# Delta-rule scan of a two-block network: where a unit's first VectorE operations stand, and when masks, end-decay products, transposes and the values' product are issued

## The reference

```python
def _rwkv7_scan(r, w, k, v, kk, a):
    def step(S, inp):
        r_t, w_t, k_t, v_t, kk_t, a_t = inp
        sa = -jnp.einsum('nhvk,nhk->nhv', S, kk_t)
        S = S * w_t[:, :, None, :] + sa[..., None] * (kk_t * a_t)[:, :, None, :] + v_t[..., None] * k_t[:, :, None, :]
        return S, jnp.einsum('nhvk,nhk->nhv', S, r_t)
```

## Time and profile before

| | us |
|---|---|
| median of 3 runs | 2951.4 |
| lowest, highest | 2947.35, 2955.93 |
| profiled execution, its time | 2956.71 |
| profiled execution, its span | 2954.9 |
| the scan of the delta rule, from about 455 to 700 of the span | 245 |

### The profile page before, as it was taken

The page is one execution under the profiler, slowest core; times in us unless marked ns, Lnnn a source line. Parts: engine busy times, 40 slices in busy tenths (PEclk is TensorE's granted clock), DMA queues, the critical chain, the costliest instruction groups (busy, mean ns, idle before and its releaser), DMA issues.

```text
span 2954.9 us, 41669 instructions
## 1 busy us (share of the span) xinstructions
PE 2779.1 (94%) x16834; PEld 2127.0 (72%) x16834; DVE 1735.8 (59%) x3143; ACT 1140.5 (39%) x2006; POOL 209.1 (7%) x212
## 2 busy tenths in 40 slices
PE   7999897789999999999988998999999998999998
PEld 4888766775666666666645776888888775788887
DVE  4256886565767777767647787433334687443333
ACT  3332244222256556555622327422223327432222
POOL 0000000000012222122200020000000030000000
PEclk9999897899999999999999999999999998999999
DMA  6210001434279889889976340323313240222412
GB/s 230 86 57 22 1 1 46 120 90 148 95 266 346 345 339 349 337 333 356 356 290 244 97 111 1 117 62 122 100 68 128 91 116 12 86 80 73 140 55 74
DMA packets 186541, 442.37 MB, mean 150 GB/s; under 512 B 21283, under 2 KB 110694, under 8 KB 167014
## 3 DMA queue, kind: packets, MB, share of 16 engines
q1 hardware_dynamic: 161862, 396.59, 37.3%
q0 software_dynamic: 24480, 43.04, 4.9%
HBM read 426.43 MB, written 38.29 MB: 157 GB/s over the span
## 4 chain that ended last, share of the span: by engine, by line
PE 78%; DVE 9%; DMA 7%; ACT 4%; issue 2%; POOL 0%; SPq 0%; POOLq 0%; DVEq 0%; ACTq 0%
PE ps L296 18%; PE ps L298 18%; PE ps L297 18%; PE ps L2502 6%; DMA hg<-h_rows,idx 3%; PE ps L2018 2%; DMA ring<-in_ew 2%; PE ps L1509 2%; PE ps L2528 2%; PE ps L2741 1%; DVE Pb L3488 1%; PE ps L2222 1%; PE ps L3393 1%; PE ps L586 1%; DMA yr<-y_rows 1%
## 5 line engine op out<-in xcount | busy, mean ns | idle before, releaser
L2953 DVE TENSOR_TENSOR wf<-ring,wf 128x1024 fp32r<-128x1024 f32 (+1 forms) x152 | 181.7, 1197 | 310.5 <-ACT wf L2949 310.1
L2949 ACT ACTIVATE wf<-ring 128x1024 fp32r<-128x1024 f32 (+1 forms) x152 | 156.8, 1033 | 343.3 <-PE ps L298 343.3
L296 PE MATMUL ps<-hxh,wf 128*128 128x512 f32 (+1 forms) x736 | 280.6, 381 | 2.3 <-DVE hxl L3116 2.3
L297 PE MATMUL ps<-hxl,wf 128*128 128x512 f32 (+1 forms) x736 | 280.3, 381 | 0.0
L298 PE MATMUL ps<-hxh,wf 128*128 128x512 f32 (+1 forms) x736 | 280.2, 381 | 0.0
L2440 DVE TENSOR_TENSOR spA<-ring,spA 128x1024 fp32r<-128x1024 f32 x156 | 184.7, 1221 | 105.5 <-ACT spA L2435 104.8
L2502 PE MATMUL ps<-ring,hdT 128*128 128x512 f32 x520 | 239.5, 604 | 0.8 <-issue 0.8
L2435 ACT ACTIVATE spA<-ring 128x1024 fp32r<-128x1024 f32 x156 | 158.3, 1055 | 53.0 <-DMA ring<-in_ew 42.5
L2502 PEld LDWEIGHTS ps<-ring,hdT 128*128 128x128 f32 x520 | 95.6, 194 | 97.2 <-issue 94.8
L2440 DVE TENSOR_TENSOR spB<-ring,spB 128x1024 fp32r<-128x1024 f32 x104 | 124.1, 1222 | 69.5 <-ACT spB L2435 69.5
L296 PEld LDWEIGHTS ps<-hxh,wf 128*128 128x128 f32 x736 | 139.1, 189 | 28.7 <-DVE hxl L3116 2.8
(11 more groups left out here) (621 smaller groups left out, 6181.7 us busy)
## 6 DMA issues: line engine op xcount, KB each, us to landing
ring<-in_ew SPq DMA_DIRECT2D x65, 2048.0 KB
ring<-in_ew SPq DMA_DIRECT2D x65, 1024.0 KB
ring<-in_w_in SPq DMA_DIRECT2D x17, 2048.0 KB, 8.9
ring<-in_w_gate SPq DMA_DIRECT2D x20, 1024.0 KB, 5.5
ring<-in_w_up SPq DMA_DIRECT2D x20, 1024.0 KB, 8.0
ring<-in_w_down SPq DMA_DIRECT2D x16, 1024.0 KB, 5.0
adaw<-in_ada_w SPq DMA_DIRECT2D x24, 512.0 KB, 6.2
ring<-in_w_out SPq DMA_DIRECT2D x6, 2048.0 KB, 8.1
```

Of the source, the lines that this page charges most:

```text
L296: pe.matmul(o, lhs[0], rhs[0], start=start, stop=False)
L297: pe.matmul(o, lhs[0], rhs[1], start=False, stop=False)
L2949: act.activation(item_part(n)[0], item_raw(n), ACT.Copy).then_inc(*w_hi.inc(n))
L2953: v.tensor_tensor(item_part(n)[1], item_raw(n), f(item_part(n)[0]), ALU.subtract).then_inc(*w_lo.inc(n))
```

## The change

Three edits, in DVE's, PE's and ACT's parts of the scan:

- `id` and `r0` of unit i+1 are issued on DVE at the end of unit i, in each direction's last step, right behind its `yo`. Before, each direction issued them at the head of unit i+1, ahead of its own `AT`. Unit 0's stand behind its `rows`.
- The masks `Bm`, `Ab`, `Ak` and the products `od2`, `od3` are issued on DVE behind level 1 instead of ahead of it.
- On PE the transposes `tr` follow U2 instead of U1, and `bv` follows U3 instead of U2; the copies on ACT move with them (`opE`, `opO` behind X2, `bv` behind X4).

```diff
-    q_pe = [Signal(sem(f"rw_mm{d}"), rw_keys(d, "c", "p2 p3 X1 U1 tr X2 U2 bv X3 U3" + " X4 U4" * d,
+    q_pe = [Signal(sem(f"rw_mm{d}"), rw_keys(d, "c", "p2 p3 X1 U1 X2 U2 tr X3 U3 bv" + " X4 U4" * d,
...
-    q_act = [Signal(sem(f"rw_scalar{d}"), rw_keys(d, "e ep dt", "X1 opE opO X2 X3 bv" + " X4" * d, "X4 " * (1 - d) + "X5 u0 TK")) for d in range(2)]
+    q_act = [Signal(sem(f"rw_scalar{d}"), rw_keys(d, "e ep dt", "X1 X2 opE opO X3" + " X4 bv" * d, "X4 bv " * (1 - d) + "X5 u0 TK")) for d in range(2)]
...
-                if k == 1:
+                if k == 2:
                     pe.wait_ge(*PV.val((u, "od3")))
...
-                if k == 2:
+                if k == 3:
                     pe.wait_ge(*PA.val((u, "opE")))
...
-                if k == 3:
+                if k == 4:
                     act.wait_ge(*P.val((u, "bv")))
...
-                if k == 1:
+                if k == 2:
                     act.wait_ge(*P.val((u, "tr")))
...
+        def start(i):
+            u, pu = (i, d), (i - 1, d)
+            if i:
+                v.wait_ge(*P.val((pu, "TK")))
+            v.tensor_copy(four(TT), bcm(C("cid"), 4)).then_inc(*PV.inc((u, "id")))
+            if i >= 2:
+                if i > 2:
+                    v.wait_ge(*P.val((pu, "y1")))
+                v.tensor_tensor(OPC[:, 0, :, :], rwm[:, 0:2, ORD[d][i] * 128:(ORD[d][i] + 1) * 128], E3[:, :, 0, :],
+                                ALU.mult).then_inc(*PV.inc((u, "r0")))
         v.wait_ge(*z_act.val("gsq"))
         rows(0)
+        start(0)
         yield
...
-            if i:
-                v.wait_ge(*P.val((pu, "TK")))
-            v.tensor_copy(four(TT), bcm(C("cid"), 4)).then_inc(*PV.inc((u, "id")))
-            if x:
-                if i > 2:
-                    v.wait_ge(*P.val((pu, "y1")))
-                v.tensor_tensor(OPC[:, 0, :, :], rwm[:, 0:2, tok], E3[:, :, 0, :], ALU.mult).then_inc(*PV.inc((u, "r0")))
...
             yield
-            mask(1, 1, f"ce_{d}", BTm, "Bm")
-            if x:
-                mask(0, 0, f"ci_{d}", Abt, "Ab")
-                mask(1, 0, f"ci_{d}", Akt, "Ak")
-            v.wait_ge(*PA.val((u, "dt")))
...
             yield
             for k in range(1, 6):
                 if k < 5:
                     aof(k + 1)
                 level(k)
                 yield
+                if k == 1:
+                    mask(1, 1, f"ce_{d}", BTm, "Bm")
+                    if x:
+                        mask(0, 0, f"ci_{d}", Abt, "Ab")
+                        mask(1, 0, f"ci_{d}", Akt, "Ak")
+                    v.wait_ge(*PA.val((u, "dt")))
...
                 if k < 5:
                     yield
...
+                if n and i < 5:
+                    start(i + 1)
                 yield
```

More of the change, by code:

```diff
@@ L1486, in rw_keys @@
         return out
-    q_pe = [Signal(sem(f"rw_mm{d}"), rw_keys(d, "c", "p2 p3 X1 U1 tr X2 U2 bv X3 U3" + " X4 U4" * d,
+    q_pe = [Signal(sem(f"rw_mm{d}"), rw_keys(d, "c", "p2 p3 X1 U1 X2 U2 tr X3 U3 bv" + " X4 U4" * d,
                                                 "X4 U4 " * (1 - d) + "X5 U5 u0 TK sa0 h0 ~y0 sa1 h1 ~y1"))
             for d in range(2)]
-    q_act = [Signal(sem(f"rw_scalar{d}"), rw_keys(d, "e ep dt", "X1 opE opO X2 X3 bv" + " X4" * d, "X4 " * (1 - d) + "X5 u0 TK")) for d in range(2)]
-    q_dve = [Signal(sem(f"rw_vector{d}"), rw_keys(d, "k1 k2 k3", "id ~r0 AT T0 TT0 Tm0 A1 Bm ~Ab ~Ak od2 od3 A2 TT1 Tm1 A3 TT2 Tm2 A4 TT3 Tm3 "
+    q_act = [Signal(sem(f"rw_scalar{d}"), rw_keys(d, "e ep dt", "X1 X2 opE opO X3" + " X4 bv" * d, "X4 bv " * (1 - d) + "X5 u0 TK")) for d in range(2)]
+    q_dve = [Signal(sem(f"rw_vector{d}"), rw_keys(d, "k1 k2 k3", "id ~r0 AT T0 TT0 Tm0 A1 A2 TT1 Tm1 Bm ~Ab ~Ak od2 od3 A3 TT2 Tm2 A4 TT3 Tm3 "
                                                   "A5 TT4 Tm4 TT5", "sa0 hq0 hd0 sa1 hq1 hd1 ~yo")) for d in range(2)]
@@ L1752, in rw_dve @@
                 yield
+                if k == 1:
[4 more added lines that the diff above has]
+                    v.wait_ge(*PA.val((u, "dt")))
+                    for a in range(2):
+                        v.tensor_tensor(OPD[:, a, :, :].rearrange("p q (c t) -> p (q c) t", c=2),
+                                        OPC[:, 2 + a, :, :].rearrange("p q (c t) -> p (q c) t", c=2), bc(Dt[:, i % 2, :], 64),
+                                        ALU.mult).then_inc(*PV.inc((u, f"od{2 + a}")))
                 if k < 5:
```

## The result

| | before | after |
|---|---|---|
| median, us | 2953.52 (6 runs, 2947.35 to 2958.59) | 2934.23 (6 runs, 2930.6 to 2936.48) |
| ratio to before, 95% interval | | 0.9942 [0.9927, 0.9956] |
| span of the profiled execution | 2954.9 | 2928.8 |
| the scan in that profile, `Tm0` of d = 1 in unit 0 to the last `yo` | 234.71 | 215.77 |

The changed kernel is faster: 17 us by the ratio, 13 to 22 by its interval (19 by the two medians). The forecast was 12.0 us and 2939.4, so the sign and the place were right and the gain was larger than forecast: it lies above the interval of 9 to 16 us that the prediction's main case gave. In the two profiles the scan alone is 18.9 us shorter.

A forecast was written before the change was run, and what follows sets the result against it. It took the hand-over between DVE and PE at the unit heads as the bound. Heads 15.2 us less 3.2 for levels 1 to 3 gave 12.0, from a median of 2951.4 to 2939.4 us; range 2932 to 2947.

The forecast's parts named there:

- the prediction's main case: Whole kernel: 12.0 us gained, 2939.4 us; interval 9 to 16 us, chance 0.61.
- What bounds the kernel: Unit heads: neither engine full; PE waits 16.1 us for r0 and 11.1 for A1, a hand-over between DVE and PE.
- the order is worth nothing: Rival: PE's work bounds the stretch, 198 of 245 us busy, so the time stays 2951; chance 0.06.
- The heads: Start of each unit: early id and r0 shorten the hand-over, 15.2 us gained over all units.
- Levels 1 and 2: Per unit, 9.83 us before: 9.0 at full clock, gain 0.8; 10.4 at half clock, loss 0.6.
- Level 3: Per unit: bv behind U3 delays d = 1 by 0.65 and exceeds TT3 and Tm3 by 0.26, loss 0.9 us.
- -3.2 us for levels 1 to 3 in units 2 to 5: Loss of 0.8 us in each of four units, with half of the units at the half clock.
- Units 0 and 1, taken at 0: Levels there: unit 1 +1.2 us at full clock or -1.5 at half, unit 0 1.5 either way; both counted as 0.
- The clock never falls: Rival: PE's clock stays full in the scan, 16.7 us gained, 2934.7 us; chance 0.08.
- Levels give more back: Rival: clock falls in every unit, levels cost 2.5 us a unit, 5 us gained, 2946 us; chance 0.20.
- The clock stays down to the unit's end: Rival: clock falls at the head and stays low, +12.8 us a unit, 2987 us; chance 0.05.
- What would show it: Trace after: r0 wait under 3 us, masks and bv on the chain, scan's end some 12 us earlier.

The follow-up runs named there:

- start_d0: The changed kernel with id and r0 of d = 1 put back at the unit's head; ratio to before 0.9979, scan 226.10 us.
- after_fill2: The changed kernel with unread products on PE in units 2 to 5, three and five; ratio to before 0.9931, scan 216.75 us.
- before_fill2: The kernel before with unread products, 9 and 5, behind PE's rows at heads of units 2 to 5; ratio 0.9987, scan 230.05 us.

## Why the prediction was right, and where it was off

**What bounds the kernel: right.** The hand-over between DVE and PE at the head, not either engine's load. The rival that said that the order is worth nothing, because PE bounds the stretch, fell: no product was taken away and the kernel gained 17 us. I had put it down to the Trainium skill's rule for the most occupied engine ("Perfetto Trace Analysis", "Identifying the Most-Contended Engine"), and that read too much into it. The section says which engine to work on first, and for TensorE it wants MFU and the share of the weight loads, not of the matmuls. By that share PE comes first here too, at 175 of 245 us against DVE's 155. It doesn't say that such an engine's waits for another are worth nothing, and the gain did come out of PE's waits: the 27 us for `r0` and `A1` are 13.6 after. DVE's instructions were only the means.

**The heads: right, and close unit by unit.** The gain in the table above stands in the row of the unit before.

| head of unit | 1 | 2 | 3 | 4 | 5 | sum |
|---|---|---|---|---|---|---|
| forecast, us | 0.2 | 3.2 | 3.8 | 3.3 | 4.5 (3.8) | 15.0 (of 15.2; unit 0's 0.2 lies ahead of the scan) |
| measured, us | 0.19 | 3.42 | 3.91 | 4.01 | 4.55 | 16.1; 15.9 with -0.14 in unit 5's own end |

Unit 3's stretch from the last y to X1 was forecast at 5.7 us and is 5.64. `start_d0` shows the reason given for it, that d = 1's rows hide behind `AT` to `A1` of d = 0: with only that half undone 10.3 us come back. Taken from the last y to X1 of d = 1 alone, unit 3 gained 3.9 and unit 4 3.5 (621.17 to 630.19 before, 609.38 to 614.87 after). Unit 2, from its state update to X1, took 6.58 us instead of 10.7, 4.2 gained: its rows ran at the full clock (1.14 us), for which the prediction had 3.9. That the table's 3.42 lies by the 3.2 of the half clock is luck; 0.7 were lost earlier in that step, 0.3 of them in a longer pause of PE (0.72 against 0.44).

**Levels 1 and 2: the sum was right, the weights were not.** At the full clock 9.0 was forecast, and unit 2 has 8.92 from X1 of d = 1 (540.16) to X3 (549.08). At the half clock 10.4 was forecast, and unit 3 has 9.73 (577.18 to 586.91), because the clock was back after 3 us, not after the whole two levels. The masks are on the chain and the transposes off it, as said. Three things were off. Where I took the clock to fall in half of the units, it fell in one of units 2 to 5 in the first profile (unit 3) and in units 3 and 5 in the second. Where it fell, the unit was still 0.1 shorter than before in levels 1 and 2, and not 0.6 longer. And I took unit 3, 9.83 us, for all units of before; by the transposes unit 3 has 10.09, and units 2 and 5 10.35 and 10.37, so they had more to gain (1.2 each).

**Level 3: the mechanism was right, the size twice too large.** 0.9 us a unit forecast, 0.47 measured in units 1 to 4 and none in unit 5; unit 0, taken at nothing, grew by 2.2. I had priced the eight products at a group of their own (0.65) on d = 0 plus 0.26 on d = 1. Back to back with U3 they cost 0.47, and d = 1's are hidden.

**The term of the sum that failed is -3.2 us for levels 1 to 3 in units 2 to 5.** Measured from the table: +0.70, -0.38, +0.27 and +1.19, together +1.8, which is 5.0 us better. Units 0 and 1, taken at 0, gave +0.4 and +0.8. With 0.7 more from the heads that is the 6.9 us between 12.0 forecast and 18.9 in the scan. The kernel's ratio puts the whole at 17 [13, 22], so the forecast lies 1 us below the interval. The measured median, 2934.23, lies in the range of 2932 to 2947 because its lower end was set for the rival in which the clock never falls, and what carried the time there was in part another thing, the levels' sign. That much was luck; the heads, 15.9 of the 18.9 us, for the most part were not.

**The rivals.** "The clock never falls", 16.7 us, is nearest in size, but not in its reason: `after_fill2` is that case, made true, and gained nothing over the change. With the clock full throughout, levels 1 to 3 of its units 2 to 5 are 2.6 us shorter than before, where the rival's sum had them 0.4 longer. What I had missed was more in the size of the levels than in the clock. "Levels give more back" is refuted: no unit of the kernel after has levels 1 and 2 longer than before, in either profile, and with level 3 the worst is unit 3 with 0.4 us lost, not 2.5. "The clock stays down to the unit's end" is refuted: the clock is 1.00 from 580 to the end of unit 3. What I held for certain and was wrong is that the half clock is dear in the old order; `before_fill2`, which kept it up most of the time, shows 4 us for the whole kernel.

**What would show it.** The wait for `r0` under 3 us: it is 0.7. `bv` on the chain in level 3: yes. All behind the scan shifted by the same: the load behind it moved from 699.69 to 678.49, 21.2 us, of which the scan explains 18.9 and the work ahead of it 2.3. `ada`'s loads were costed at nothing; its 64 products stand at the same step, and no wait for a load is among PE's largest waits.

## What to carry to other kernels

Where two engines hand work to each other and neither is full, read the chain at the hand-over in the order of one queue: two directions woven to cover each other may run one behind the other because a short instruction of the second stands behind the long steps of the first. Moving that instruction ahead, to where its engine rests, was worth 14 of the 17 us here (14.5 of 18.9 in the scan). Before moving work off the chain, name what it was covering: masks, transposes and `bv` each came back at about their price when moved once more. And price a slow stretch of one engine by what else stands on the chain there, not by the ratio of its lengths.

## What the runs showed of the hardware beyond what I expected

- The half clock cost less than its ratio. A block pair took 1.98 at 0.50 and 1.16 at 1.00, yet raising the mean clock from 0.87 to 0.97 with unread products was worth 4.7 us of 234.7 in the old order, since DVE's masks then stand on the chain, and from 0.99 to 1.00 nothing in the new.
- Shorter waits didn't keep the clock up everywhere. With no wait for DVE at the heads above 1.6 us (PE's waits of after) it still fell in unit 3 of both profiles of the kernel after; it was back at 580, with PE busy 2.8 of 3.0 us ahead of that, where before it stayed down for 10 us with PE busy 6.65 of 10.7.
- PE pauses of 0.3 to 0.7 us inside a row of products, which the profile names "issue", with no wait for another engine. In unit 5 of the kernel after, PE's row products are in two pieces:

```profile
645.53 0.66 PE ps L1541 x14
...
646.80 0.88 PE ps L1541 x18
```

  The first ends at 646.19, so 0.6 us lie between. They come at different places in different kernels. The fourteen profiles hold 26 of over 0.3 us in the scan, and every one begins 1.6 to 2.3 us behind the start of a load on the queue that brings instructions (`q8 instruction` on the page; 36 or 37 loads between 455 and 700, one in 6.7 us). That the two go together the traces show; that the load causes the pause no run here tests. Together they are 0 to 2.7 us of a scan, so they can be part of why two profiles differ.
